# Two attention outputs turned by VectorE block transposes and a DRAM scratch in place of TensorE transposes

## What is computed

```python
h = x @ w_in[l]
rq, rk, rv, rg, cq, ck, cv, dq, dk, dv, gates = split(h)
o_a = silu(rg) * rms_norm(retention(rq, rk, rv))               # (256, 1024), 4 heads of 256
o_b = chunk_attention(cq, ck, cv)                              # (256, 512)
o_c = rms_norm(diff_attention(dq, dk, dv, lam)) * (1 - init)   # (256, 512), 4 heads of 128
g = sigmoid(gates + b_merge[l])
merged = g[0] * (o_a @ w_branch_a[l]) + g[1] * (o_b @ w_branch_b[l]) + g[2] * (o_c @ w_branch_c[l])
x = layer_norm(ALPHA * x + merged @ w_out[l])
x = layer_norm(ALPHA * x + (silu(u_gate) * u_up) @ w_ffn_out[l])   # u = x @ w_ffn_in[l]
```

## Time and profile before

| | |
|---|---|
| median of 3 runs | 2306.23 us (2305.64 to 2306.27) |
| the profiled execution, its own time | 2305.94 us |
| its span, first to last instruction | 2304.2 us |
| instructions | 30370 |
| granted TensorE clock | 1.000 |
| HBM read and written | 441.76 MB and 18.35 MB |

### The profile page before, as it was taken

One profiled execution on the slowest core, in us unless ns is written; L12 is line 12 of the kernel. 1 busy time (PEld: TensorE's weight loads), 2 busy tenths in 40 slices (PEclk: granted clock), 3 DMA queues, 4 the chain that ended last, 5 costly groups with the idle time before them and its releaser, 6 DMA issues.

```text
span 2304.2 us, 30370 instructions
## 1 busy us (share of the span) xinstructions
PE 2295.8 (100%) x11304; PEld 1919.0 (83%) x11304; DVE 1506.7 (65%) x2381; ACT 1234.1 (54%) x1910; POOL 127.7 (6%) x141
## 2 busy tenths in 40 slices
PE   9999999999999999999999999999999999999999
PEld 8888888888888888888888888888888888888887
DVE  6656786565567866576487765664766587657654
ACT  6555544445556354455467654554554478555443
POOL 3130000004210000000000000000000000000000
PEclk9999999999999999999999999999999999999999
DMA  8455468755454587577654444875677544456772
GB/s 336 162 190 169 171 218 291 229 184 182 149 198 165 167 287 243 191 239 248 196 188 153 159 155 165 262 245 190 220 246 238 179 163 156 152 172 206 234 235 89
DMA packets 165456, 462.10 MB, mean 201 GB/s; under 512 B 18880, under 2 KB 53312, under 8 KB 164288
## 3 DMA queue, kind: packets, MB, share of 16 engines
q1 hardware_dynamic: 165312, 460.18, 59.8%
HBM read 441.76 MB, written 18.35 MB: 200 GB/s over the span
## 4 chain that ended last, share of the span: by engine, by line
PE 96%; DVE 2%; DMA 1%; ACT 0%; issue 0%; DVEq 0%
PE bank L2003 28%; PE bank L2008 27%; PE bank L2007 27%; PE bank L2060 3%; PE bank L1990 2%; PE bank L1991 2%; PE bank L1992 2%; DMA raw<-in_weights 1%; DVE wl L1531 1%; PE bank L2149 1%; PE bank L2111 0%; PE bank L2134 0%; PE bank L2082 0%; DVE x L1721 0%; PE bank L2151 0%; ACT wh L1303 0%
## 5 line engine op out<-in xcount | busy, mean ns | idle before, releaser
L1303 ACT ACTIVATE wh<-raw 128x1024 fp32r<-128x1024 f32 (+1 forms) x778 | 814.3, 1052 | 787.4 <-PE bank L2008 716.1
L1531 DVE TENSOR_TENSOR wl<-raw,wh 128x1024 fp32r<-128x1024 f32 (+1 forms) x778 | 928.8, 1224 | 293.9 <-ACT wh L1303 289.9
L2003 PE MATMUL bank<-wh,xh 128*128 128x512 f32 (+1 forms) x2102 | 827.5, 394 | 1.4 <-DVE xl L1560 0.9
L2008 PE MATMUL bank<-wh,xl 128*128 128x512 f32 (+1 forms) x2102 | 816.1, 388 | 0.0
L2007 PE MATMUL bank<-wl,xh 128*128 128x512 f32 (+1 forms) x2102 | 815.0, 388 | 0.0
L2003 PEld LDWEIGHTS bank<-wh,xh 128*128 128x128 f32 x2102 | 394.7, 188 | 82.3 <-issue 3.2
L2008 PEld LDWEIGHTS bank<-wh,xl 128*128 128x128 f32 x2102 | 394.5, 188 | 81.3
L2007 PEld LDWEIGHTS bank<-wl,xh 128*128 128x128 f32 x2102 | 395.0, 188 | 76.5
L2003 PE MATMUL bank<-wh,act_h 128*128 128x512 f32 x528 | 206.0, 390 | 0.0
L2008 PE MATMUL bank<-wh,act_l 128*128 128x512 f32 x512 | 199.3, 389 | 0.0
L2007 PE MATMUL bank<-wl,act_h 128*128 128x512 f32 x512 | 199.3, 389 | 0.0
(11 more groups left out here) (351 smaller groups left out, 2079.7 us busy)
## 6 DMA issues: line engine op xcount, KB each, us to landing
raw<-in_weights SPq DMA_DIRECT2D x760, 512.0 KB, 4.2
turn<-ffn_s SPq DMA_DIRECT2D x264, 64.0 KB, 2.8
ffn_a<-turn SPq DMA_DIRECT2D x66, 256.0 KB, 4.7
raw<-in_weights SPq DMA_DIRECT2D x16, 384.0 KB, 3.2
ln<-in_ln SPq DMA_DIRECT2D x4, 1024.0 KB, 7.0
bias<-in_bias SPq DMA_DIRECT2D x2, 1024.0 KB, 9.2
b_merge<-in_b_merge SPq DMA_DIRECT2D x2, 1024.0 KB, 5.5
gain<-in_gain_ffn SPq DMA_DIRECT2D x4, 512.0 KB, 3.7
```

Source lines behind the costliest of these rows:

```text
L1303: act.activation(wh[:, u % NH, 0:used(u)], raw[:, u % NR, 0:used(u)], ACT.Copy).then_inc(hi_done, 1)
L1531: dve.tensor_tensor(wl[:, u % NR, 0:used(u)], raw[:, u % NR, 0:used(u)], wh[:, u % NH, 0:used(u)].bitcast(F32), ALU.subtract).then_inc(lo_ ...
L2003: pe.matmul(out, h, w_h, start=st.first and i == 0, stop=False)
L2008: last = pe.matmul(out, lo, w_h, start=False, stop=ends)
```

## The change

The `split` steps of `rg` and `dq` go, and with them `split_rows`. For each of three pieces (`rg0` and `rg1`, the two row tiles of `rg`, and `oc`, both tiles of `dq`) come four steps:

- `block`: DVE transposes the piece in 32x32 blocks (one instruction of 128x1024 for each of `rg0` and `rg1`, two of 128x512 for `oc`) into a staging place: `rv` for the first two, `cv` for `oc`
- `out`: SP waits for it and writes it to DRAM with four DMAs of 128 KB, in runs of 1 KB
- `back`: SP waits until these four have landed and reads all 512 KB back with one DMA, into `rg` or `cv`
- `halve`: ACT waits for it and writes the high part (128x1024); DVE subtracts to get the low part

The steps stand at these places: `block` of both rg pieces at 28, `out` at 29 and 30, `back` at 31 and 32, `halve` at 33 and 34; for `oc` 55, 57, 59 and 62. The DVE part of `halve` of `rg0` also waits until `rg1` has been written out, since `oa_l` lies over its staging place. All other side steps keep their places. The units of `w_branch_a` and `w_branch_c` wait on the semaphore `halved`.

```diff
-UNITS_AMONG_1 = "41011100011000010101113201120100110103021301123110021010102011207"
+UNITS_AMONG_1 = "41011100011000010101113201120100110100011111130112311002101010201102232"
...
+    def moved(self, what, name, **kw):
+
+        if what == "block":
+            kw["n"] = self.of_block[name] = self.count("blocked")
+        elif what == "out":
+            kw["n"] = self.of_block[name]
+        elif what == "copy":
+            kw["n"] = self.count("copied")
+        elif what == "halve":
+            kw["n"], kw["m"] = self.count("hi"), self.count("halved")
+        self.add(what, name=name, **kw)
+        return kw.get("m") or kw.get("n")
...
-    def split_rows(src, dst, nkt, rows=None):
-        for r in range(R):
-            last = p.next_t()
-            for kg in range(0, nkt, 4):
-                if kg:
-                    last = p.next_t()
-                p.add("split", t=last, src=src, dst=dst, tile=r, kg=kg, scale=1.0, rows=rows, n=p.count("hi"))
-        return last
...
     p.add("ret_fin", rows=p.count("rows"), o=p.o - 1)
+    for r in range(R):
+        h_a = p.moved("block", f"rg{r}", rows=p.cc["rows"], dst="oa", tile=r)
     p.add("load", name="bm12", s=ret_s3, roped=roped)
     p.add("load", name="ln1", roped=roped)
-    t_a = split_rows("rg", "oa", KT, rows=p.cc["rows"])
-
+    for r in range(R):
+        h_a = p.moved("out", f"rg{r}", rows=p.cc["rows"], dst="oa", tile=r)
+    for r in range(R):
+        h_a = p.moved("back", f"rg{r}", rows=p.cc["rows"], dst="oa", tile=r)
+    for r in range(R):
+        h_a = p.moved("halve", f"rg{r}", rows=p.cc["rows"], dst="oa", tile=r)
...
     p.add("da_fin", rows=p.count("rows"), o=p.o - 1)
     da_rows = p.cc["rows"]
-    t_c2 = split_rows("dq", "oc", 4, rows=p.cc["rows"])
+    for what in ("block", "out", "back", "halve"):
+        h_c = p.moved(what, "oc", rows=da_rows, dst="oc")
     side = p.begin()
     for j in range(2):
-        merge(0, j, "w_branch_a", "oa", KT, t_a, j)
+        merge(0, j, "w_branch_a", "oa", KT, j, after_h=h_a)
...
-        c = p.chunk(("w_branch_c", [(512 * j, 512 * j + 512)]), "oc", 4, 512, j, t_c2)
+        c = p.chunk(("w_branch_c", [(512 * j, 512 * j + 512)]), "oc", 4, 512, j, None, after_h=h_c)
...
+        stage = {"rg0": b["rv"][:, 0, :],
+                 "rg1": b["rv"][:, 1, :],
+                 "oc": b["cv"][:, :, :].rearrange("p r n -> p (r n)")}
+        landed = {**stage,
+                  "rg0": b["rg"][:, 0, :],
+                  "rg1": b["rg"][:, 1, :]}
...
+                    elif st.kind == "out":
+                        sp.wait_ge(blocked, st.n)
+                        to = a["moved"][MOVED.index(st.name)].rearrange("(q j b n) -> b j q n", q=4, j=32, b=4)
+                        for k in range(4):
+                            sp.dma_start(to[k], stage[st.name][32 * k:32 * k + 32, :].rearrange("p (q n) -> p q n", q=4))\
+                              .then_inc(moved_out[st.name], 16)
+                    elif st.kind == "back":
+                        sp.wait_ge(moved_out[st.name], 64 * (st.l + 1))
+                        sp.dma_start(landed[st.name], a["moved"][MOVED.index(st.name)].rearrange("(p n) -> p n", p=P))\
+                          .then_inc(moved_back[st.name], 16)
...
+                    elif k == "halve":
+                        act.wait_ge(moved_back[st.name], 16 * (st.l + 1))
+                        h, source = split_of[st.dst][0], landed[st.name].rearrange("p (b m n) -> p m b n", b=4, m=8)
+                        if st.dst == "oc":
+                            h = h.rearrange("p k (r b n) -> p (k r) b n", r=R, b=4)
+                        else:
+                            h = h[:, :, st.tile * P:st.tile * P + P].rearrange("p k (b n) -> p k b n", b=4)
+                        act.activation(h, source, ACT.Copy).then_inc(t_hi, 1)
...
+                    elif k == "block":
+                        if st.name in ("rg0", "rg1"):
+                            dve.wait_ge(rows, st.rows)
+                            last = dve.transpose(stage[st.name].rearrange("p (q m n) -> p q m n", q=4, m=8),
+                                                 b["rg"][:, st.tile, :].rearrange("p (m q n) -> p q m n", m=8, q=4))
+                            last.then_inc(blocked, 1)
+                            continue
...
+                        to = stage[st.name].rearrange("p (q k r n) -> p q k r n", q=4, k=4, r=R)
+                        for r in range(R):
...
+                                part = b["dq" if st.name == "oc" else st.name][:, r, :]
+                            last = dve.transpose(to[:, :, :, r, :], part.rearrange("p (k q n) -> p q k n", k=4, q=4))
+                        last.then_inc(blocked, 1)
...
+                    elif k == "halve":
+                        dve.wait_ge(t_hi, st.n)
+                        if st.name == "rg0":
+                            dve.wait_ge(moved_out["rg1"], 64 * (st.l + 1))
+                        h, lo = split_of[st.dst]
+                        source = landed[st.name].rearrange("p (b m n) -> p m b n", b=4, m=8)
+                        if st.dst == "oc":
+                            h, lo = [w.rearrange("p k (r b n) -> p (k r) b n", r=R, b=4) for w in (h, lo)]
+                        else:
+                            h, lo = [w[:, :, st.tile * P:st.tile * P + P].rearrange("p k (b n) -> p k b n", b=4) for w in (h, lo)]
+                        dve.tensor_tensor(lo, source, h.bitcast(F32), ALU.subtract).then_inc(halved, 1)
...
+                        if st.after_h:
+                            pe.wait_ge(halved, st.after_h)
...
+    a["moved"] = nc.dram_tensor("moved", (len(MOVED), P * D), F32, kind="Internal").ap()
```

More of the change, by code:

```diff
@@ L78, with __init__ @@
 class Step:
-    def __init__(self, kind, after_a=0, after_o=0, after_t=None, apart=None, apply=None, b=None, c=None, dst=None, early=None,
+    def __init__(self, kind, after_a=0, after_c=0, after_h=0, after_o=0, after_t=None, apart=None, apply=None, b=None, c=None, dst=None, early=None,
                  end=None, fed=None, first=None, form=None, g=None, gate=None, h=None, half=None,
@@ L88, in __init__ @@
         self.after_a = after_a
+        self.after_c = after_c
+        self.after_h = after_h
         self.after_o = after_o
@@ L157, in __init__ @@
         self.pair = 0
+        self.of_block = {}
     def add(self, kind, **kw):
@@ L213, in next_d, with unit @@
         return self.d[pair] - 1
-    def unit(self, w, lhs, kt0, nk, n, pair, nth, first, last, after_t, form="rows", after_o=0, stacked=None, after_a=0):
+    def unit(self, w, lhs, kt0, nk, n, pair, nth, first, last, after_t, form="rows", after_o=0, stacked=None, after_a=0,
+             after_h=0):
         u = len(self.units)
@@ L218, in unit, with chunk @@
         self.add("unit", u=u, lhs=lhs, kt0=kt0, nk=nk, n=n, pair=pair, nth=nth, first=first, last=last,
-                 after_t=after_t, form=form, after_o=after_o, stacked=stacked, after_a=after_a)
+                 after_t=after_t, form=form, after_o=after_o, stacked=stacked, after_a=after_a,
+                 after_h=after_h)
         return u
-    def chunk(self, w, lhs, nkt, n, pair, after_t, form="rows", after_o=0, among=None):
+    def chunk(self, w, lhs, nkt, n, pair, after_t, form="rows", after_o=0, among=None, after_h=0):
         nth = self.next_d(pair)
@@ L227, in chunk @@
         for i, (k0, nk) in enumerate(groups):
-            u = self.unit(w, lhs, k0, nk, n, pair, nth, i == 0, i == len(groups) - 1, after_t, form, after_o)
+            u = self.unit(w, lhs, k0, nk, n, pair, nth, i == 0, i == len(groups) - 1, after_t, form, after_o, after_h=after_h)
             if among:
@@ L255, in pass_first @@
                          first=st.first, last=st.last, after_t=lead[0] if lead else st.after_t, stacked=st.stacked,
-                         after_a=st.after_a, tiles=(0,), apart=apart)
+                         after_a=st.after_a, after_h=st.after_h, tiles=(0,), apart=apart)
                 if apart:
@@ L392, in gate, with merge @@
         p.add("gate", c=c, b=b, j=j, n=g_of[b, j])
-    def merge(b, j, w, lhs, nkt, t_l, pair, after_o=0):
-        c = p.chunk((w, [(512 * j, 512 * j + 512)]), lhs, nkt, 512, pair, t_l, after_o=after_o)
+    def merge(b, j, w, lhs, nkt, pair, after_o=0, after_h=0):
+        c = p.chunk((w, [(512 * j, 512 * j + 512)]), lhs, nkt, 512, pair, None, after_o=after_o, after_h=after_h)
         p.add("merge", c=c, b=b, j=j, n=g_of[b, j])
@@ L450, in plan_block1 @@
     for j in range(2):
-        merge(1, j, "w_branch_b", "ob", 4, None, j, ob_o + 1)
+        merge(1, j, "w_branch_b", "ob", 4, j, ob_o + 1)
     p.weave(before, dense_a + p.begin(), side, UNITS_AMONG_1)
@@ L882, in at @@
         return self.nc.alloc_sbuf_tensor_at(name, list(shape), dt, offset=self.base + offset), offset + size
+MOVED = ('rg0', 'rg1', 'oc')
 GAIN0 = {"gain_ffn1": 1, "gain_m": 2, "gain_ffn2": 3}
@@ L966, in build @@
         act_split = sem("act_split")
```

(31 more changed lines are left out.)

## The result

The changed kernel takes 2310.09 us (median of 20 runs, 2307.3 to 2314.25) against 2306.22 us (20 runs, 2305.64 to 2307.59): a ratio of 1.0018, with a 95% interval of 1.0012 to 1.0024. That is 3.9 us more: a small loss, clear of the noise, inside the 0.2% that the prediction counts as no change, 9 us above its forecast and 4.1 us above the end of its range (2306.0). The profiled execution took 2308.39 us of its own, 2.45 more than that of the kernel before, for a span of 2306.7.

What follows compares the result with a forecast made beforehand. The prediction took PE's own instruction stream to bound the kernel. It summed 2305.94 - 5.36 (transposes) + 0.2 (waits) = 2300.8 us, or 2301.1 against the median, the forecast; range 2300.2 to 2306.0.

Steps and rivals of the forecast that it cites:

- What leaves PE: Transposes of `rg` and `dq` on PE: removing them saves 2.68 us a layer, 5.36 us in two, counted in full.
- rival of the full duration: The 48 transposes hold PE for their full duration, 13.3 us, so the result is 2292.9; chance 0.02.
- Blocks: DVE's two 128x1024 block transposes of `rg`: 1.2 us each from 168.0, done at 169.2 and 170.4.
- Halves: ACT's and DVE's halves of `rg`, 1.15 us each: for rg1 from 181.0 to 182.15, then to 183.3.
- 0.25 us to spare: First `w_branch_a` unit: rg1's low half done at 183.3, PE wants it at 183.56, so no wait.
- Out: SP's writes of `rg` to DRAM: rg0 issued to 171.0, rg1 171.5 to 173.2; rg0 complete at 173.7.
- Back: Reads of `rg` from DRAM through the full queue, 1.27 us per 512 KB: rg0 lands at 178.5, rg1 at 181.0.
- short-wait rival: At the first `w_branch_a` unit, two hops 1 us slower each: PE waits 1.9 us a layer, 2304.7; chance 0.30.
- `oc`: Trip of `dq`: `back` lands before 262, low half done at 269.1, PE starts at 270.24; no wait, 1.1 us to spare.
- Cover: DVE's 3.1 us more a layer is hidden by an 18 us lead; the delayed weight load lands by 174.7, in time for ACT.
- rival of the extra work: DVE's additional 3.1 us a layer reaches PE whole through late `wl`: 2307.1, no change; chance 0.05.
- The long wait: At the first `w_branch_a` unit, behind full queues, PE waits 5.5 us a layer: 2311.9, slower; chance 0.07.

Runs made afterwards that it cites:

- e3: Changed kernel without `out` and `back` of `rg`; ACT takes its halves straight from `rg`, and DVE no longer waits for `out` of rg1: 2301.33 us, 0.9979.
- e7: Changed kernel with the edits of e5 and e6 together: 2300.70 us, 0.9977.
- e2: Changed kernel with `rg` turned on TensorE again, so that only `dq` makes the trip through DRAM: 2305.53 us, 0.9998.
- e8: Changed kernel without `out` and `back` of rg1, whose halves are taken from `rg` as it stands; only rg0 makes the trip: 2302.69 us, 0.9988.
- e9: Changed kernel without the writes of rg0 and rg1; each `back` reads a unit of weights, and DVE's wait for `out` of rg1 goes: 2301.56 us, 0.9981.
- e1: Changed kernel with the 2 MB loads `bm12` and `ln1` sent behind the trip of `rg` and no longer ahead of it: 2308.05 us, 1.0008.
- e5: Changed kernel with other places: both `out` at 29, both `back` at 30, both `halve` at 33, no weight load within either pair: 2302.31 us, 0.9985.
- e6: Changed kernel where PE takes the first `w_branch_a` chunk's four units by row tile, tile 0 (needing only rg0) before tile 1: 2301.78 us, 0.9983.
- e4: Changed kernel with 22 matmuls of 256 columns that nobody reads, ahead of the first unit that reads `oa`: 2306.78 us, 1.0003.

## Why the prediction was wrong, point by point

*What leaves PE*: right. -5.36 is confirmed by e3 (forecast 2301.1, 2301.33) and by e7. The rival of the full duration is out.

*Blocks*: right. Two take 2.36 us (1.2 each), from 168.1. *Halves*: right in size. ACT's take 1.06, DVE's 1.23, together 0.04 us more than reckoned from the landing of rg1 to the end of its low half (186.03). The tanh starts at 176.28, 0.84 later than before; the 0.9 was right, though 2.4 less 1.2 is 1.2. But one term was left at nothing: from the end of the low half PE needs another 0.26 us to start (186.03 to 186.29, and as much in layer 2). That alone is the 0.25 us to spare.

*Out* and *Back*: **this is the step that failed**, by the size of its terms: "a full queue moves 512 KB in 1.27 us", four times of it from 173.4 to 178.5. Forecast `back` of rg0 and rg1 at 178.5 and 181.0; measured 181.1 and 183.7. By terms: SP was through with `out` of rg1 at 174.3 instead of 173.2 (the first `out` began 0.2 late, four issues take 2.0 to 2.1 us, not 1.76, and around the weight load between them 0.3 more went by), so `back` of rg0 left 1.1 late; it took 6.2 us, not 4.7. `out` of rg1 took 4.2 us from its last issue, not 2.8, and `back` 5.6, not 5.0. The 1.27 was read off weight loads and charged for a queue that also carries writes in packets of 1 KB, and that SP feeds with gaps. Over the trip it was 1.54, and 2.2 in the 3.9 us that begin with `out` of rg0 (238 GB/s). So 2.7 us of lateness, 0.04 of the halves and 0.26 of PE's start, less the 0.25 to spare and 0.07 by which PE itself comes later, make the wait of 2.66 (2.93 in layer 2). It is the short-wait rival's mechanism and place, at 1.5 times its size. The prediction's own sign, "wrong if that landing is later than 181.3", came true: it was 183.7.

The Trainium skill ("DMA: Bandwidth & Descriptors", the anatomy of one DMA) gives a transfer issued by GpSimd about 2 us of fixed cost, for the most part the receipt of the last write, besides its bytes. For a piece of 128 KB an estimate by that page is 2.3 us. SP issues the ones here, for which that section has no figure; the first `out` of a layer, with 2.7, are near the estimate all the same. Those of rg1, with 4.1, are not, nor are the `back` (3.2 by the page, 5.6 to 6.2 measured). What they take beyond it is put down here to the queue.

*The clock behind the wait*: not in the prediction at all, neither in the forecast nor in the price of a rival. A wait of 1.9 us was charged with 1.9. It is 3.0 to 3.3 us of the median, more than one of the waits. With the measured waits and the clock the sum is 2300.9 + 5.6 + 3.0 to 3.3 = 2309.5 to 2309.8, against 2310.09. Without the clock it would have been 2306.5, 1.8 above the short wait's 2304.7. The two hold-ups and the price of the clock are read off single traces and set beside medians, so the agreement to 0.6 us is partly luck.

*`oc`*: the conclusion was right (e2, and 1.36 us between the low half and PE in the changed kernel; forecast 1.1), but one step not: `back` left at 260.0 and landed at 266.7 instead of before 262. It didn't matter, since ACT came to its half at 268.8 only.

*Cover*, and the rival of the extra work: it cost nothing, as e7 carries all of it at 2300.70. DVE's busy time rose by 3.3 us on the page for both layers together (1506.7 to 1510.0), not by 3.1 a layer. The weight load that SP held up went at 171.81 and landed at 176.4, 1.7 later than forecast, and still before ACT's `hi` at 177.24. *The long wait*: did not come, but 2.7 to 2.9 us lay about halfway between the two rivals.

*"Against it: the account already uses the full queue"* was the poor argument by which the short wait got 0.30 and not more: the account used a full queue of one kind of transfer. With 0.25 us to spare and two hops uncertain by 1 us each, the two cases deserved equal chances at best.

Open stays why the queue is slow behind the first `out`: the write, its small packets, or SP, which feeds it with gaps (0.5 us of the 1.6 by the shares). A run with the writes in place and the held-up loads sent before them would tell. Also open are the waits of a few tenths that shift between executions; they blur each figure here by 0.5 to 1 us, and e2 and e8 lost about 1 us that their edits don't explain. e3 and e9 have, like e2, 0.3 to 0.4 us more outside the span than the kernel before.

## What to carry to other kernels

When a step is moved from the bounding engine to a trip through DRAM, time the trip in the queue that it shares, with its own packets and its own issue times in it: 512 KB took 1.54 us over this trip, where loads alone take 1.27. If the margin is smaller than that uncertainty, first let the consumer ask for one tile at a time (worth 8.3 us of the median here) or put the trip's pieces next to each other (7.8 us), and only then count the gain. Price a wait of some 2 us on TensorE with the half clock behind it, and look for it in the granted clock of a narrow window, since the page of 40 slices shows all nines.

## What the hardware showed unexpectedly

- A wait of 2.1 to 2.8 us at PE was followed by a granted clock of one half in three of four cases (both layers of e1, layer 2 of the changed kernel), at 1.4 to 1.7 us each (1.4 from the intervals in the changed kernel; in e1 18 us by a clock that is 0.09 down, rounded); one of 0.9 us (e5) and a hold-up of 0.26 us (e6) were not. 22 matmuls that nobody reads kept the clock at 2.4 GHz and so saved 3.0 to 3.3 us.
- The DMA queue carried 238 GB/s over 3.9 us with four writes of 128 KB ahead of a weight load, and 410 without writes; three slices of 0.3 us were down to 181, 55 and 150. Four more writes of the same size, a little later and with the queue well filled, went at 379.
- From the end of DVE's low half to PE's first matmul that needs it 0.25 to 0.26 us pass when PE stands waiting (changed kernel, both layers, and e5).
- The changed kernel's times spread more: 7 us between the lowest and the highest of 20 runs, against 2 us before. That the wait does it isn't shown: with the wait filled (e4) it is 2.5 us over 11 runs, but in e6, where PE hardly waits, 4.2.
